# Delta rule's inverse on one Trainium2 core: T from its transpose by VectorE's 32x32 block transpose on levels 0 to 4

## The reference, cut to what matters

```
a_low = jnp.where(strict, jnp.einsum('nbhik,nbhjk->nbhij', kb, kc) * decay, 0.0)
m = a_low + jnp.eye(c, dtype=F32)
u = lax.linalg.triangular_solve(m, vb, left_side=True, lower=True, unit_diagonal=True)
w = lax.linalg.triangular_solve(m, kb * jnp.exp(G)[..., None], left_side=True, lower=True, unit_diagonal=True)
```

## Time and profile before

| what | value |
|---|---|
| median of 3 runs | 994.96 us (989.38 to 996.2) |
| span of the profiled execution | 987.1 us |
| instructions | 12455 |
| busy: PE, PEld, DVE, ACT, POOL | 93%, 51%, 40%, 18%, 22% of the span |

### The profile page before, as it was taken

One profiled execution on the slowest core, in us unless ns is written; L12 is line 12 of the kernel. 1 busy time (PEld: TensorE's weight loads), 2 busy tenths in 40 slices (PEclk: granted clock), 3 DMA queues, 4 the chain that ended last, 5 costly groups with the idle time before them and its releaser, 6 DMA issues.

```text
span 987.1 us, 12455 instructions
## 1 busy us (share of the span) xinstructions
PE 915.9 (93%) x5024; PEld 499.0 (51%) x5024; DVE 398.7 (40%) x824; ACT 178.8 (18%) x316; POOL 217.5 (22%) x322
## 2 busy tenths in 40 slices
PE   8999988998997999899989779999879999999992
PEld 5888867986353433333333267844434333333330
DVE  4599418726645122122234169702552121211225
ACT  0411231223020111101101153301301111111111
POOL 4679983301020511101100020100112001110000
PEclk9999997999997999999999999999979999999997
DMA  9456639102769879999999927570398999999952
GB/s 271 111 174 241 245 136 302 63 12 99 259 213 407 324 287 357 402 413 408 402 403 425 421 114 215 181 302 1 139 410 340 390 406 399 403 405 407 411 248 88
DMA packets 83420, 277.28 MB, mean 281 GB/s; under 512 B 25240, under 2 KB 44134, under 8 KB 60694
## 3 DMA queue, kind: packets, MB, share of 16 engines
q1 hardware_dynamic: 70298, 255.86, 67.4%
q10 hardware_dynamic: 10660, 16.49, 5.2%
q0 software_dynamic: 2400, 4.07, 1.4%
HBM read 260.97 MB, written 18.01 MB: 283 GB/s over the span
## 4 chain that ended last, share of the span: by engine, by line
PE 80%; DMA 10%; DVE 5%; ACT 2%; issue 2%; POOL 0%; SPq 0%; DVEq 0%; ACTq 0%
PE ps L1844 20%; PE ps L342 12%; PE ps L1868 10%; PE ps L2524 6%; DMA ring<-in_moe_w_up 5%; PE ps L1886 5%; DMA x_rows<-work 4%; PE ps L1791 4%; PE ps L804 3%; PE ps L2386 1%; PE ps L305 1%; PE ps L1480 1%; PE ps L633 1%; PE ps L650 1%; PE ps L2401 1%
## 5 line engine op out<-in xcount | busy, mean ns | idle before, releaser
L1844 PE MATMUL ps<-ring,work 128*64 128x512 f32 x416 | 187.9, 604 | 5.5 <-DMA ring<-in_moe_w_up 4.1
L1845 PE MATMUL ps<-ring,work 128*64 128x512 f32 x416 | 187.9, 604 | 0.0
L1928 DVE TENSOR_TENSOR work<-ps,work 64x512 f32<-64x512 f32 x32 | 33.8, 1055 | 208.8 <-ACT work L1899 208.8
L342 PE MATMUL ps<-work,ring 128*128 128x264 f32 x512 | 115.2, 387 | 0.0
L1844 PEld LDWEIGHTS ps<-ring,work 128*64 128x64 f32 x416 | 55.5, 139 | 115.8 <-issue 107.0
L1868 PE MATMUL ps<-ring,work 128*64 128x512 f32 x216 | 100.0, 606 | 6.8 <-issue 5.4
L342 PEld LDWEIGHTS ps<-work,ring 128*128 128x128 f32 x512 | 96.8, 190 | 16.4
L1869 PE MATMUL ps<-ring,work 128*64 128x512 f32 x216 | 100.1, 607 | 0.0
L1249 POOL TENSOR_TENSOR ring<-ring 128x512 f32<-128x512 f32 (+5 forms) x76 | 90.4, 1208 | 9.5 <-DVE ring L1245 6.2
L1938 DVE COPY work<-ps 64x512 f32<-64x512 f32 x32 | 22.2, 694 | 156.9 <-PE ps L1869 156.9
L1949 POOL COPY work<-work 64x1 int32<-64x1 int32 x30 | 5.8, 194 | 319.3 <-PE ps L1791 277.3
(11 more groups left out here) (490 smaller groups left out, 1276.2 us busy)
## 6 DMA issues: line engine op xcount, KB each, us to landing
ring<-in_moe_w_down SPq DMA_DIRECT2D x27, 2048.0 KB, 19.5
ring<-in_moe_w_gate SPq DMA_DIRECT2D x52, 1024.0 KB, 15.5
ring<-in_moe_w_up SPq DMA_DIRECT2D x52, 1024.0 KB, 17.7
ring<-in_w_in ACTq DMA_DIRECT2D x6, 2048.0 KB, 8.9
work<-in_moe_w_gate SPq DMA_DIRECT2D x12, 1024.0 KB, 17.0
work<-in_moe_w_up SPq DMA_DIRECT2D x12, 1024.0 KB, 19.1
work<-in_moe_w_down SPq DMA_DIRECT2D x5, 2048.0 KB, 25.5
s_out_mats<-ring SPq DMA_DIRECT2D x4, 1280.0 KB, 4.8
```

The source lines that it names most:

```text
L342: last = nc.tensor.matmul(ps[:, proj_bank(j), 0:T], win[g % 2][:, k, (j % 4) * P:(j % 4 + 1) * P], xT[:, k], start=k == 0, stop=k == DC - 1)
L1844: nc.tensor.matmul(ps[0:SLOT, 5, :], xgT[s][:, c], gate_w[slot][:, c], start=c == 0, stop=c == DC - 1)
L1845: last = nc.tensor.matmul(ps[SLOT:P, 5, :], xgT[s][:, c], up_w[slot][:, c], start=c == 0, stop=c == DC - 1)
L1928: nc.vector.tensor_tensor(hid[s][0:SLOT].rearrange("t (c p) -> t p c", c=4), strided(ps[SLOT:P, 5, :]), strided(sg[s][SLOT:P]), ALU.mult). ...
```

## The change

On levels 0 to 4 the group L646, the TensorE transposes L625 and the subtractions L917 and L932 go. In their place VectorE transposes `tinvT` in 32x32 blocks, each block in its own place, into `tinv`; since T's blocks have at most 32 rows up to level 4, this is the whole transpose there. The instruction for a tile follows that tile's subtraction in VectorE's queue and waits for it. Level 5 keeps its three groups. GpSimd's wait for the transposes of level 0 goes as well.

```
         def gdn_pe_level(t, b):
 
             if b == 0:
-                for i in range(TT):
-                    t.wait_ge(*dv.at(f"level0.{i}"))
-                    for h in range(H):
-                        last = nc.tensor.transpose(bank4(4 + i)[:, h], at_lev[0][:, 4 * i + h], ident)
-                    last.then_inc(*pe.done(f"z0.{i}"))
                 return
...
                 t.wait_ge(*dv.at(f"tinvT{b - 1}.{i}"))
-                if b < 6:
+                if b == 5:
                     for h in range(H):
...
+        def tinv_turned(v, b, i):
+
+            v.wait_ge(*dv.at(f"tinvT{b}.{i}"))
+            mine = slice(4 * i, 4 * i + 4)
+            nc.vector.transpose(flat(tinv[:, mine]), flat(tinvT[:, mine])).then_inc(*dv.done(f"tinv{b}.{i}"))
+
...
             for i in range(TT):
-                v.wait_ge(*pe.at(f"z0.{i}"))
-                nc.vector.tensor_tensor(tinv[:, 4 * i:4 * i + 4], unit, bank4(4 + i), ALU.subtract).then_inc(*dv.done(f"tinv0.{i}"))
-            for i in range(TT):
                 v.wait_ge(*dv.at(f"level0.{i}"))
                 mine = slice(4 * i, 4 * i + 4)
                 nc.vector.tensor_tensor(tinvT[:, mine], unit, at_lev[0][:, mine], ALU.subtract).then_inc(*dv.done(f"tinvT0.{i}"))
+            for i in range(TT):
+                tinv_turned(v, 0, i)
...
                     mine = slice(4 * i, 4 * i + 4)
-                    if b < 6:
+                    if b == 5:
                         v.wait_ge(*pe.at(f"tz{b}.{i}"))
                         nc.vector.tensor_tensor(flat(tinv[:, mine]), flat(tinv[:, mine]), banks(2 + i), ALU.subtract).then_inc(*dv.done(f"tinv{b}.{i}"))
                     v.wait_ge(*pe.at(f"zt{b}.{i}"))
                     nc.vector.tensor_tensor(flat(tinvT[:, mine]), flat(tinvT[:, mine]), banks(4 + i), ALU.subtract).then_inc(*dv.done(f"tinvT{b}.{i}"))
+                    if b < 5:
+                        tinv_turned(v, b, i)
...
-                if b >= 2:
+                if b > 2:
                     pool.wait_ge(*pe.at(f"z{b - 2}.1"))
```

## The result

The changed kernel takes 982.55 us (median of 6 runs, 976.55 to 985.95) against 995.24 (6 runs of the kernel before, 989.38 to 997.73). The profiled execution took 976.55 us, its span is 974.8, against 987.1 before.

The account below looks back on a forecast made before the run. VectorE's queue was taken to bound levels 0 and 1, TensorE levels 2 to 5. A loss of 0.2 us and 5.1 us saved made 4.8 us off 994.96: 990.1, range 985.2 to 997.5.

Parts of the forecast that it names:

- The transpose's price: One VectorE transpose of 128x512 float32 was taken at 0.69 us, like a pass of that shape; bounds 0.6 to about 1.2.
- Rival 3: Ten transposes on VectorE's chain stream slower than a pass; over 1.17 us decides, at 1.38 the time is 997.1; 12%.
- Levels 2 to 4: Without L646 the period falls to 4.88 us a level, three periods from 19.71 to 14.64: 5.1 us saved.
- The ring that was worked out: At levels 2 to 4, VectorE's subtractions and transposes plus TensorE's next first group close a period of 4.88 us.
- rival 2: Transposes collide with GpSimd's masks, 3.0 us at levels 2 to 4, up to 1.4 at level 0: gain 0.4, 994.6; 20%.
- rival 4: TensorE's new gaps at levels 2 to 4 bring its clock to 1.2 GHz: 9 us slower in all, 1004; 3%.
- Levels 0 and 1: VectorE's queue stays the bound there, so TensorE's removed work gains nothing and 0.2 us is lost.
- L923 meets the masks of level 2 as it does now: At level 0, VectorE's L923 overlaps GpSimd's masks as before the change, so its time was left unchanged.
- the 32-column instruction: VectorE's L1022, slowed to 1.18 us by GpSimd, was counted 0.3 us quicker as masks come earlier.
- Rival 1: TensorE stays the bound from level 0 on, so all work leaving it counts: 9.5 us gained, 985.5; 8%.
- The mixer's gain: Level 5's L646 starts at 193.12 in place of 197.95, 4.8 us earlier, taken off the whole time.
- What the mixer gains is therefore handed on: From the mixer's last product to the kernel's end, the 4.8 us passes on; no transfer behind starts by another clock.

Follow-up runs that it names:

- experiment 7: The changed kernel with every VectorE transpose done twice, the second waiting for the first: 988.49 us, ratio 0.9953 against the kernel before.
- Experiment 10: The changed kernel with level 0 put back as before (TensorE transposes, subtractions from PSUM), levels 1 to 4 as changed: 983.01 us, ratio 0.9884 against the kernel before.
- experiment 9: The changed kernel with VectorE's attention mask and q-decay products (L923, L925) moved behind level 5: 979.01 us, ratio 0.9852 against the kernel before.
- Experiment 5: The changed kernel plus 36 tiny unread products (144 instructions) in TensorE's idle stretch at level 0: 990.49 us, ratio 0.9968 against the kernel before.
- experiment 6: The kernel before plus 28 tiny unread products (112 instructions) ahead of level 0's transposes: 988.45 us, ratio 0.9948 against the kernel before.
- the repeat: The changed kernel run again without an edit, next to the kernel before on one chip: 981.75 us, ratio 0.9895.
- experiment 3: The kernel before with six unread 128x512 products more on TensorE ahead of the mixer's output projection: 993.87 us, ratio 1.0012 against the kernel before.

## Why the prediction was wrong, point by point

**The transpose's price** was right: 0.69 taken, 0.706 measured, with 0.6 to 1.2 as bounds. The estimate by the Trainium skill (VectorE: DVE Perf Modes, "The three transpose paths"), 0.71, was the nearer one. Rival 3 had the right mechanism for a dearer transpose: in experiment 7 the doubled one closes a period of 6.39 us. Its condition, a transpose over 1.17, did not hold.

**Levels 2 to 4** were right: 4.88 us a level forecast, 4.90, 4.98 and 4.93 measured. The ring that was worked out is the bound at level 2; at levels 3 and 4 it is TensorE's own queue, for which the prediction had 4.87. The transposes didn't collide with GpSimd, though several lie inside its masks (both of level 0 and tile 0's of level 2), so rival 2 fell. The clock stayed at 1.00 in all three windows, so rival 4 fell. Its ground, that the clock falls after idle times of over 2 us alone, did not hold: at level 0 it fell 0.2 us after TensorE's last product.

**Levels 0 and 1** were right in sum and wrong in a detail. "L923 meets the masks of level 2 as it does now" failed: it took 2.29, not 1.21, L925 stayed at 1.75, and the 32-column instruction that got 0.3 us of relief got all of its 1.0. VectorE was free at 174.56, forecast 174.8; level 2's last group began at 178.24, forecast 178.48. But this profile enters the stage 0.4 us earlier (VectorE's L908 at 160.35, now L909 at 159.96), so by its own length the stage lost 0.4 us for a forecast of 0.2. Experiment 10 puts level 0's part at a gain of 0.3, which leaves a loss of 0.7 for level 1. Rival 1 needed VectorE free some 2 us earlier; experiment 9 brought that about by another edit, and then TensorE was the bound there as the rival said.

**The mixer's gain** was right: 4.8 forecast, 4.78 in the chain, 4.4 if the stage's entry, 0.4 us earlier in the profile after, is taken off. Experiment 5, which has the changed levels with the code length of before, measures the term by itself: 0.9968 (0.9939 to 0.9997), 3.2 us with an interval of 0.3 to 6.1.

**The step that failed** is the one from there to the end of the kernel: "What the mixer gains is therefore handed on; I find no transfer behind it that starts by another clock." The chain and the queue's wait show that a delay in the mixer is handed on; they don't show that nothing else is changed behind it. What starts by another clock there is a transfer all the same, the one that fetches TensorE's code, and the sum priced the 144 removed instructions by their time alone and not by their place in the code. The kernel before had the sign of it: the chain had an "issue" of 2.75 us at the last experts, and page part 3 lists the queue. Without any change in the mixer, experiment 6 gains 0.9948 (0.9923 to 0.9973), 5.2 us with an interval of 2.7 to 7.7. The profiles name 2.6 us of it at the last experts, 1.9 in layer 1's rows and 0.9 up to layer 0's rows (31.9 against 31.0), less 0.9 that come back behind layer 1's rows: 4.5 together.

**What is still open.** The mixer's 4.8 and the code's 4.5 are 9.3 us, of 10.9 (8.1 to 13.9) by the ratio and 12.7 by the medians. The profiled pair has 2.3 us up to layer 0's rows, and the repeat only 1.2 of it. That wait follows the code as well: the six profiles with 24 to 168 more instructions have 31.3 to 31.9 us, the other seven 29.6 to 31.0. In the six a packet of 16 KB starts between 1.1 us before and 3.2 us after the start of the transfer that the chain shows, in the others none between 8.9 before and 16.2 after. For layer 1's slow rows it starts between 3.6 us before and 3.0 after, in the others none between 11.8 before and 15.6 after. The rest, and the small median of experiment 3, are of the size of the runs' own spread of 4 to 10 us. Two stretches of low clock that some profiles have and others don't are of that size too: one at the kernel's start, in six profiles, worth 1.4 to 3.0 us, and one between the last experts of layer 0 and the end of S5, in five, worth 1.4 to 3.3 us. What sets them off isn't shown.

## What to carry to other kernels

Work out a change in the middle of a long program from its own ring of waits, as here; it held within 0.1 us a level. Where two bounds come out level, as here, look in the profile after which of them it is. But instructions removed or added also move all code behind them: before a gain or a loss far from the edit is explained by queues, look for waits of "issue" next to a packet of the instruction queue, and undo the shift alone, with the same number of idle instructions in a gap. Whether a kernel has such a wait is then chance, and 112 useless instructions in the right place brought this one 5 us.

## What the runs showed of the hardware that was not expected

- A product group behind a late packet of code starts 2.6 to 2.7 us after that packet of 16 KB (five profiles, 2.62 to 2.70), and the wait stands as "issue", up to 3.9 us. That the packet brings this group's code is read from experiments 5 and 6; no view names what it holds.
- A VectorE transpose of 128x512 float32 in 32x32 blocks takes 0.71 us, as long as a subtraction of that shape (0.69), also beside GpSimd's masks (0.71 at 180.17, and 1.29 for the two of level 0).
- L923, with both inputs in SBUF, took 1.21 us where it started 0.25 us before GpSimd's masks (before), and 2.29 where it started inside them (after). L925 took 1.75 inside them in both, and 0.67 away from them (experiment 9).
- A 16 KB packet of code also delays other transfers: of 13 profiles, the five that have one near the start of layer 1's rows need 17.8 to 18.1 us for them, the others 15.9 to 16.2.
